# State-space scan: one exponential per direction from a running sum and a per-token offset, masks added on GpSimd, X left unweighted, parts from the states scaled on VectorE

## The reference

```python
xc = (x * dt[..., None]).reshape(bsz, nc, CHUNK, g, r, p)      # 8 chunks of 128 tokens, 4 groups of 6 heads of 64
a = (dt * A).reshape(bsz, nc, CHUNK, g, r).transpose(0, 3, 4, 1, 2)
a_cum = jnp.cumsum(a, axis=-1)
lmat = jnp.exp(segsum(a))                                      # exp(cum[l] - cum[s]) for s <= l, else 0
cb = jnp.einsum('bclgn,bcsgn->bgcls', cc, bc)
y_diag = jnp.einsum('bgcls,bgrcls,bcsgrp->bclgrp', cb, lmat, xc)
...
y_off = jnp.einsum('bclgn,bcgrpn,bgrcl->bclgrp', cc, prev_states, jnp.exp(a_cum))
y = (y_diag + y_off).reshape(bsz, length, g, r, p)
```

## Time and profile before

| what | value |
|---|---|
| median of the runs | 3125.96 us |
| span of the profiled execution | 3120.8 us |
| TensorE busy | 2782.4 us (89%) |
| VectorE busy | 2201.9 us (71%) |
| ScalarE busy | 1268.5 us (41%) |
| GpSimd busy | 771.4 us (25%) |
| loads of the running sums, 768 KB each | 32 |

### The profile page before, as it was taken

How to read it: one execution, slowest core, us unless ns; L and a number is a source line. 1 busy time by engine, 2 the same in 40 slices (tenths; PEclk the granted TensorE clock), 3 DMA queues, 4 the chain that set the end, 5 groups by cost and what they waited for, 6 DMA issues and landing times.

```text
span 3120.8 us, 35706 instructions
## 1 busy us (share of the span) xinstructions
PE 2782.4 (89%) x13124; PEld 2228.8 (71%) x13124; DVE 2201.9 (71%) x2958; ACT 1268.5 (41%) x2069; POOL 771.4 (25%) x389
## 2 busy tenths in 40 slices
PE   6999999989588869979979996989899589999998
PEld 3777776765366658867867884777788468888887
DVE  5599976525688944854644898974465469999997
ACT  2222221110166641123224314666532057777775
POOL 1422220000111100000210005555300036666564
PEclk9999999999788879989989998999999689999999
DMA  6233338643544452226544237341232279999996
GB/s 222 89 108 125 112 118 273 210 150 104 182 165 182 172 213 89 79 78 147 101 119 97 94 89 161 110 120 25 89 122 97 115 285 383 383 382 384 386 383 223
DMA packets 245383, 543.43 MB, mean 174 GB/s; under 512 B 31125, under 2 KB 155141, under 8 KB 228946
## 3 DMA queue, kind: packets, MB, share of 16 engines
q1 hardware_dynamic: 175234, 437.01, 39.6%
q0 software_dynamic: 33680, 58.97, 7.7%
q10 hardware_dynamic: 36288, 45.09, 4.1%
HBM read 450.74 MB, written 108.06 MB: 179 GB/s over the span
## 4 chain that ended last, share of the span: by engine, by line
PE 49%; DVE 8%; POOL 2%; DMA 2%; ACT 2%; issue 1%; SPq 1%; DVEq 0%; ACTq 0%; POOLq 0%; another core or an unknown queue 0%
PE banks L143 44%; PE banks L153 4%; DVE c_rows L1512 2%; DVE a_P L2151 1%; POOL a_P L2175 1%; ACT a_PT L2194 1%; DVE m_w_low L1610 0%; DVE e_low L2654 0%; DMA ofoxT<-a_o 0%; POOL a_R L1545 0%; DMA i_q<-iqT 0%; DVE a_R L1550 0%; ACT m_w_low L1603 0%; DMA p_low_raw<-in_w_out 0%; DMA odsaT<-a_o 0%
## 5 line engine op out<-in xcount | busy, mean ns | idle before, releaser
L2654 DVE TENSOR_TENSOR e_low<-e_raw,e_high 128x4096 fp32r<-128x4096 f32 x99 | 437.9, 4425 | 64.2 <-ACT e_high L2648 64.1
L143 PE MATMUL banks<-m_w_low,p_high 128*128 128x512 f32 (+1 forms) x1280 | 391.7, 390 | 8.5 <-DVE m_w_low L1610 8.5
L2648 ACT ACTIVATE e_high<-e_raw 128x4096 fp32r<-128x4096 f32 x99 | 359.5, 3634 | 27.0 <-DVE e_g L2603 26.9
L143 PE MATMUL banks<-h_high,w 128*128 128x512 f32 (+1 forms) x1088 | 309.3, 368 | 9.0 <-POOL w L373 4.4
L143 PEld LDWEIGHTS banks<-m_w_low,p_high 128*128 128x128 f32 x1280 | 240.0, 194 | 53.0 <-issue 8.7
L143 PE MATMUL banks<-m_w_low,p_low 128*128 128x512 f32 (+1 forms) x640 | 247.2, 386 | 0.0
L143 PEld LDWEIGHTS banks<-h_high,w 128*128 128x128 f32 x1088 | 195.4, 190 | 49.0 <-POOL w L373 4.8
L143 PE MATMUL banks<-e_high,e_xhigh 128*128 128x512 f32 x528 | 211.5, 401 | 7.3 <-issue 5.5
L504 DVE SCALAR_TENSOR_TENSOR acc<-img,taps,acc 128x1024 f32<-128x1024 f32 x160 | 209.8, 1311 | 5.7
L143 PE MATMUL banks<-e_high,e_xlow 128*128 128x512 f32 x528 | 208.3, 394 | 0.0
L143 PE MATMUL banks<-e_low,e_xhigh 128*128 128x512 f32 x528 | 207.8, 394 | 0.0
(11 more groups left out here) (496 smaller groups left out, 6394.9 us busy)
## 6 DMA issues: line engine op xcount, KB each, us to landing
e_raw<-in_exp_w SPq DMA_DIRECT2D x99, 2048.0 KB, 13.9
s_sums<-cumT SPq DMA_DIRECT2D x32, 768.0 KB, 4.3
w_raw<-in_w_in SPq DMA_DIRECT2D x20, 1024.0 KB, 6.5
s_X<-xtok SPq DMA_DIRECT2D x19, 1024.0 KB, 7.3
p_raw<-in_w_in SPq DMA_DIRECT2D x18, 1024.0 KB, 7.0
xbcT<-res ACTq DMA_DIRECT2D x20, 640.0 KB, 2.9
xtok<-xt ACTq DMA_DIRECT2D x20, 640.0 KB, 4.1
w_raw<-in_ada_w SPq DMA_DIRECT2D x12, 1024.0 KB, 5.5
```

The lines of the kernel that those rows point to most:

```text
L143: last = pe.matmul(out, a, b, start=start and n == 0, stop=stop and n == len(pairs) - 1)
L2648: act.activation(self.high[p % HIGHS][:], self.raw[p % RAWS][:], ACT.Copy).then_inc(*self.high_done.up())
L2654: dve.tensor_tensor(self.low[p % HIGHS][:], self.raw[p % RAWS][:], self.high[p % HIGHS][:].bitcast(F32), ALU.subtract).then_inc(*self.low_ ...
```

## The change

In the tables, `gap` and `back` give way to one table `off`: the logarithm of `dt` (no less than 1e-37) minus the running sum, for both directions. The scan's exponentials then take, for each direction by itself, the broadcast running sum plus `off` as bias, so that the result is already the decay times `dt` of the source token. X is used as loaded: `timed` and `xfs` go. There is no minimum of the two exponents any more; what lies outside a direction's triangle is made -1e30 beforehand, by an add of `outside` to both directions' sums on GpSimd (`shut`). The pair products are copied once, without mask, and the weights are one VectorE operation on both directions in place. `scale` moves from ScalarE to VectorE, two operations of 128x384, and gets two buffers. `sums` and `M` have three buffers. The last four steps leave out the state's update, and the last chunk its weighing. The order of the calls changes: the products from the states are made one step ahead, and a step's exponentials two steps ahead; `weights` comes ahead of `gather` and `vector_step`.

```diff
-        dve.tensor_tensor(t["gap"][:], p[:, 0:NT, 0:NH], p[:, 0:NT, NH:2 * NH], ALU.subtract).then_inc(*vec.up())
-        dve.tensor_scalar(t["back"][:], p[:, 0:NT, NH:2 * NH], -1.0, None, ALU.mult).then_inc(*self.tables_done.up())
+        dve.tensor_scalar(self.t["off"][:], self.t["dt"][:, 0:NT, :], TINY, None, ALU.max).then_inc(*vec.up())
+        act.wait_ge(*vec.at(6))
+        act.activation(self.t["off"][:], self.t["off"][:], ACT.Ln).then_inc(*self.logged.up())
...
+        dve.wait_ge(*self.logged.at(1))
+        dve.tensor_tensor(t["off"][:], t["off"][:], p[:, 0:NT, :], ALU.subtract).then_inc(*self.tables_done.up())
...
         def load_sums(n):
-            if n >= 2:
-                sp.wait_ge(*diffed.at(n - 1))
+            if n >= 3:
+                sp.wait_ge(*exped.at(n - 2))
...
+        def shut(n):
+            if n == 0:
+                for w in range(2):
+                    pool.tensor_scalar(outside[:, w, :], MASK[w], -1.0, -FAR, ALU.add, ALU.mult).then_inc(*outlined.up())
+                pool.wait_ge(*outlined.at(2))
+            pool.wait_ge(*sums_in[n % 3].at(n // 3 + 1))
+            pool.tensor_tensor(sums[n % 3][:], sums[n % 3][:], over(outside[:], 2, HG), ALU.add).then_inc(*masked.up())
+
+        def exponents(n):
+            c, g = n // NBC, n % NBC
+            act.wait_ge(*masked.at(n + 1))
+            if n >= 3:
+                act.wait_ge(*summed.at(n - 2))
             for w in range(2):
+                for h in range(HG):
+                    last = act.activation(M[n % 3][:, w, h, :], sums[n % 3][:, w, h, :], ACT.Exp, bias=col("off", c, NH * w + HG * g + h))
+            last.then_inc(*exped.up())
...
-            for w in range(2):
-                last = dve.tensor_tensor(M[n % 2][w][:], E[n % 2][:], over(cbs[c % 2][:, w, g, :], 1, HG), ALU.mult)
-            last.then_inc(*M_done.up())
+            dve.tensor_tensor(M[n % 3][:].rearrange("p w h n -> p (w h) n"), M[n % 3][:].rearrange("p w h n -> p (w h) n"), over(cbs[c % 2][:, g, :], 1, 2 * HG), ALU.mult).then_inc(*M_done.up())
...
         def scale(n):
-            act.wait_ge(*off_summed.at(n + 1))
-            if n:
-                act.wait_ge(*summed.at(n))
+            dve.wait_ge(*off_summed.at(n + 1))
+            if n >= 2:
+                dve.wait_ge(*summed.at(n - 1))
             for w in range(2):
-                for h in range(HG):
-                    at = slice(HP * h, HP * h + HP)
-                    last = act.activation(y2[w][:, at], core.bank[:, y0 + 1 + w, at], ACT.Copy, scale=col("ec", c, NH * w + HG * g + h))
+                last = dve.tensor_tensor(heads(y2[n % 2][w][:]), heads(core.bank[:, y0 + 1 + w, 0:384]), over(col("ec", c, NH * w + HG * g, HG), 2, HP), ALU.mult)
             last.then_inc(*scaled.up())
...
         def vector_step(n):
             dve.wait_ge(*stepping.at(n + 1))
+            dve.wait_ge(*off_summed.at(n + 1))
...
+        load_sums(0), load_chunk(0), load_sums(1)
...
+        load_sums(2), load_chunk(1), load_z(0)
         pool.wait_ge(*rows_in.at(2))
         dve.wait_ge(*rows_in.at(2))
+        tensor_pairs(0), from_states(0), shut(0), shut(1), skip_and_weigh(0), shut(2), skip_and_weigh(1)
+        exponents(0), exponents(1), vector_pairs(0), scale(0), weights(0)
         for n in range(N + 1):
             c, g = n // NBC, n % NBC
-            if n:
-                gather(n - 1), vector_step(n - 1)
             if n < N:
-                from_states(n), scale(n), within_chunk(n), tensor_step(n), both(n)
+                within_chunk(n)
+                if n + 1 < N:
+                    from_states(n + 1)
+                if n < STEPS:
+                    tensor_step(n)
+                both(n)
+            if n + 2 < N:
+                exponents(n + 2)
+            if n + 3 < N:
+                load_sums(n + 3), shut(n + 3)
             if n + 1 < N:
                 weights(n + 1)
-            if n + 2 < N:
-                load_sums(n + 2), differences(n + 2), exponents(n + 2)
+            if n:
+                gather(n - 1)
+                if n - 1 < STEPS:
+                    vector_step(n - 1)
+            if n + 1 < N:
+                scale(n + 1)
             if g == 0 and c:
                 gate(c - 1), roots(c - 1)
...
                 if c + 1 < NT:
                     skip_and_weigh(c + 1)
-            if g >= 2 and c + 1 < NT:
-                timed(g - 2, c + 1)
```

More of the change, by code:

```diff
@@ L995, in state_space @@
         t = {k: s.sb("s_" + k, [P, NT + NC, 2 * NH]) for k in ("dt", "ec", "dec", "et")}
-        t.update({k: s.sb("s_" + k, [P, NT, NH]) for k in ("gap", "back")})
+        t["off"] = s.sb("s_off", [P, NT, 2 * NH])
         Xs = [s.sb(f"s_X{b}", [P, DS + NBC * NST]) for b in range(2)]
@@ L1005, in state_space @@
         xb = [s.sb(f"s_xb{b}", [P, 2 * NBC, P]) for b in range(2)]
[L1006 to L1010, removed]
+        cbs = [s.sb(f"s_cb{b}", [P, NBC, P]) for b in range(2)]
+        sums = [s.sb(f"s_sums{b}", [P, 2, HG, P]) for b in range(3)]
+        M = [s.sb(f"s_M{b}", [P, 2, HG, P]) for b in range(3)]
         yts = [s.sb(f"s_y{b}", [P, DS]) for b in range(2)]
-        y2 = [s.sb(f"s_y2{w}", [P, 384]) for w in range(2)]
+        y2 = [[s.sb(f"s_y2{b}{w}", [P, 384]) for w in range(2)] for b in range(2)]
+        outside = s.sb("s_outside", [P, 2, P])
         sq, skip, nw = s.sb("s_sq", [P, 384]), s.sb("s_skip", [P, NH]), s.sb("s_nw", [P, DS])
@@ L1062, in vector_pairs @@
                 dve.wait_ge(*M_done.at(4 * c - 4))
-            for w in range(2):
[L1064 to L1073, removed]
-            for h in range(HG):
-                last = dve.scalar_tensor_tensor(out=E[n % 2][:, h, :], in0=sums[n % 2][:, 0, h, :], scalar=col("gap", c, HG * g + h),
-                                                in1=sums[n % 2][:, 1, h, :], op0=ALU.subtract, op1=ALU.min)
-            last.then_inc(*diffed.up())
+            dve.tensor_copy(cbs[c % 2][:], core.bank[:, 0, :].rearrange("p (g n) -> p g n", g=NBC)).then_inc(*cb_done.up())
@@ L1082, in exponents @@
-            for h in range(HG):
-                last = act.activation(E[n % 2][:, h, :], E[n % 2][:, h, :], ACT.Exp, bias=col("back", c, HG * g + h))
-            last.then_inc(*E_done.up())
+            act.wait_ge(*masked.at(n + 1))
+            if n >= 3:
+                act.wait_ge(*summed.at(n - 2))
+            for w in range(2):
+                for h in range(HG):
+                    last = act.activation(M[n % 3][:, w, h, :], sums[n % 3][:, w, h, :], ACT.Exp, bias=col("off", c, NH * w + HG * g + h))
@@ L1140, in both @@
             for w in range(2):
-                last = pe.matmul(core.bank[:, 2 + 3 * (n % 2), 0:384], mats[:, C_ID, :], y2[w][:], start=False, stop=w == 1)
+                last = pe.matmul(core.bank[:, 2 + 3 * (n % 2), 0:384], mats[:, C_ID, :], y2[n % 2][w][:], start=False, stop=w == 1)
             last.then_inc(*summed.up())
```

54 lines of the change are left out of this document (21 added, 33 removed).

## The result

The changed kernel takes 3143.27 us (median of four runs, 3136.76 to 3148.31) against 3125.66 in the same comparison: 1.0054 times as long, 95% interval 1.0040 to 1.0069. It is slower by 17.6 us where 4 were forecast (a forecast of 3130 in a range of 3100 to 3156). The profiled execution's span is 3135.1 us, 14.3 over before's 3120.8.

A forecast was written before the change was run, and what follows sets the result against it. VectorE, held by GpSimd, was taken to bound chunk edges, with TensorE needing 24.8 us a chunk. Entry -8.8, chunks +4.2, -2.0, +9.3, +2.2, tail -1.1 and tables 0.1 summed to +3.9: 3130 us, range 3100 to 3156.

The forecast's parts named there:

- The third stall: At a chunk's third step, TensorE waits 3.5 us for a state step delayed behind the roots' ScalarE work.
- The price of an add: GpSimd's mask add of 128x1536, once a step: 2.76 us, from the weighing's row, up to 2.9.
- A steady chunk: Scan chunk: TensorE's 24.8 us, stalls of 2.2, 1.3 and 3.5, up to 1.5 more, and a clock fall: 36.3 us.
- The slow clock: A stall over 3.4 us lets TensorE's clock fall once a chunk, costing another 3 to 4.5 us.
- Chunk 0: Scan's first chunk: GpSimd busy to 856 and stalls of 2.8 and 1.2 us, 33.8 us for 29.6, +4.2.
- rival 3: Two slow clock stretches a chunk, or the first outlasting its stall, and adds of 2.9 us: 3150 us; chance 0.22.
- Chunk 1: Scan's second chunk: no burst of adds at its start, 32.6 us for 34.5, -2.0.
- Chunks 2 to 6: Five steady scan chunks, each 1.84 us longer than before: +9.3 us.
- Chunk 7: Scan's last chunk: no state step, but burst, roots and one slow stretch, 28.8 us for 26.6, +2.2.
- Entry: Scan's start: first product at 843.6 instead of 852.39, -8.8 us.
- Rival 2: GpSimd's adds fall into gaps, only the wait for the roots is left: 29 us a chunk, about 3083; chance 0.13.
- Rival 4: VectorE's PSUM scalings are blocked too, or GpSimd keeps its turn: +40 us, 3170 us; chance 0.05.

The follow-up runs named there:

- e1: The changed kernel with GpSimd's mask add cut to 2 elements a partition, mask and decay weights left out of the result: 28.9 us a chunk.
- e2: The changed kernel with 2-element adds, each behind two GpSimd memsets that write a scratch tile without reading SBUF: 31.6 us a chunk.
- e12: The changed kernel with weights reading pairs from PSUM, state step ahead of weights, and each add in two GpSimd halves: 3084.04 us (0.9877 of before).
- e9: The changed kernel with the weights' product reading the pairs from PSUM, made in the chunk's last step, instead of an SBUF copy: 3144.97 us.
- e10: The changed kernel with pairs read from PSUM by the weights' product, and gather and state step ahead of the weights: 3079.14 us (0.9859 of before).
- e4: The changed kernel with VectorE's weights of the next step put behind gather and state step: 3124.63 us (0.9995 of before).

## Why the prediction was right on the side and short in size

**What bounds the kernel** was read rightly, and so was the path of the loss. GpSimd idle until the store lands, then operations without a gap; weights of 3 to 5 us; PSUM scalings at 0.55; stalls at the state product: all of it is in the timeline above. At the edge of chunk 3 the two state steps ended 5.5 and 16.3 us after the chunk before, where the working has 6.2 and, for the case of a third add, 16; the stalls were 1.53 and 4.62 us for 2.2 and 3.9. The third stall, 3.5 us at the third step behind the roots, did not come: TensorE, late by the second, found that state step done. A stall of 1.62 us stands at the fourth step instead, behind norm, pair copy and weights.

**The price of an add** was wrong. The forecast took 2.76 us from the weighing and set aside its other estimate, 3.4 us, which was the right one: alone an add takes 3.42, and "adds far from 2.8 us" was one of its own signs of being wrong. The weighing's second input is one value repeated over 64 elements, the add's a full row. The trace of the kernel before has such a pair at 128x2048, the first with one value for all elements and the second with a whole tile (shortest, median and longest in ns):

```profile
L371 POOL TENSOR_TENSOR w<-w_raw,zero x13: 3594/3649/3653, 52.7 to 425.9; 128x2048 fp32r<-128x2048 f32 x13
L373 POOL TENSOR_TENSOR w<-w_raw,w x13: 4492/4646/5356, 56.3 to 429.6; 128x2048 fp32r<-128x2048 f32 x13
```

The second row scaled to 1536 elements is 3.4 to 3.5 us, an estimate that could have been made beforehand. No run shows what this term cost by itself. At the edge of chunk 3 the skip product was done 1.2 us sooner than worked out, so part of the good agreement there is luck.

**A steady chunk**: 36.3 us forecast, 35.4 measured as the mean of chunks 2 to 6. Stalls of over 1 us sum to 7.6 us a chunk there, for 7.0 forecast and up to 1.5 more. The slow clock was given 3 to 4.5 us. It took 5.5 us a chunk at half speed with TensorE at work, which costs 2.7. In chunk 3 the clock is 0.52 for 5 us only and then 1.00, where before had 0.50 for 9.6. The forecast tied a slow stretch to one stall of over 3.4 us. That was wrong in itself: the clock fell behind stalls of 1.89 and 2.93 us in chunk 4 and of 2.26 us in chunk 0, and it did not behind one of 2.28 us in chunk 5.

**Chunk 0** is the term that failed most: +4.2 forecast, +11.0 measured (40.6 for 29.6). I had stalls of 2.8 and 1.2 there.

```profile
849.52 5.38 PE L1127 MATMUL banks<-s_X,s_M 128*128 128x64 f32 x24 [15.93 <-DVE s_M L1094]
...
860.67 3.37 DVE L1094 TENSOR_TENSOR s_M<-s_M,s_cb 128x1536 f32<-128x1536 f32 x1 [2.31 <-ACT s_M L1086]
...
868.47 1.62 PE L1158 MATMUL banks<-s_xd,s_X 128*128 128x384 f32 x2 [5.26 <-DVE s_H L1168]
```

They were 5.26 and 2.26 us, 3.5 more in sum. The forecast had GpSimd busy without pause to 856, some 12 us after the first product. In fact three more adds followed at once and kept it busy until 25 us after:

```profile
862.39 12.03 POOL L1076 TENSOR_TENSOR s_sums<-s_sums,s_outside 128x1536 f32<-128x1536 f32 x3
...
864.43 3.31 DVE L1166 TENSOR_TENSOR s_H<-s_H,s_et 128x384 f32<-128x384 f32 x1
...
871.00 5.03 DVE L1094 TENSOR_TENSOR s_M<-s_M,s_cb 128x1536 f32<-128x1536 f32 x1 [1.74 <-ACT s_M L1086]
```

The state step and then the weights were held by them, each ahead of a stall. The other part is the clock, for which the forecast of 33.8 us has nothing beyond before's 29.6 and the two stalls. With TensorE at work it was at half speed for 7.4 us at the chunk's start, for 5.4 after the first stall and for 3.4 after the second, 16.2 us in all where before had 8.9: another 3.7 us.

```profile
849.50:856.90 7.40, 7.38 (x28) 6.47 (x29) 4.20 (x1) 0.00 (x0) 7.40 (x2) 0.50 0.28 107
868.50:873.90 5.40, 5.40 (x13) 3.58 (x14) 3.66 (x3) 3.62 (x13) 5.40 (x2) 0.50 0.35 112
880.80:884.20 3.40, 3.40 (x7) 1.74 (x6) 3.29 (x3) 0.00 (x0) 3.21 (x1) 0.50 0.02 5
```

This is rival 3, more than one slow stretch in a chunk. Chunks 2 and 4 had two slow stretches as well, but of 3 to 4 us each, together no longer than the one that the forecast had counted.

**Chunk 1**: -2.0 forecast, +1.9 measured (36.4 for 34.6), with a stall of 4.70 us in its third step. The weights there came late behind the roots. Without the adds (e1) that leaves a stall of 2.2 us. Here the weights met the end of a single add, and the state step met the weighing:

```profile
906.41 2.15 DVE L1094 TENSOR_TENSOR s_M<-s_M,s_cb 128x1536 f32<-128x1536 f32 x1 [5.04 <-ACT s_M L1086]
...
906.89 4.28 POOL L1148 TENSOR_TENSOR s_xd<-s_X,s_dec 128x1536 f32<-128x1536 f32 x1
...
908.95 2.65 DVE L1166 TENSOR_TENSOR s_H<-s_H,s_et 128x384 f32<-128x384 f32 x1
...
912.33 1.62 PE L1158 MATMUL banks<-s_xd,s_X 128*128 128x384 f32 x2 [4.70 <-DVE s_H L1168]
```

I had taken it that without a burst there is little hold. A single instruction is enough where the state step stands behind it. What followed cost more than the stall: the clock was at half speed until 925.1, 12.8 us of TensorE's work.

```profile
912.40:925.00 12.60, 12.60 (x36) 9.23 (x37) 7.63 (x14) 3.62 (x12) 6.21 (x3) 0.50 0.39 149
```

That is the second term that failed. **Chunks 2 to 6**: +9.3 forecast, +5.0 measured. **Chunk 7**: +2.2 and +2.3. **Tail**: -1.1 and -0.85.

**Entry**: from the scan's rows landing to the first product -7.9 us (11.95 for 19.83), forecast -8.8. It didn't show in full in the span: the scan began its loads 4.3 us later, and the rows took 0.7 more to land.

```profile
823.17 0.37 SPq L1037 DMA_DIRECT2D s_sums<-cumT  x1
...
837.57 0.67 POOL L1073 TENSOR_SCALAR s_outside<-mats 128x128 f32<-128x128 f32 x2 [159.83 <-DMA s_nw<-in_ssd_norm_w]
```

In the stage ahead the granted clock from 710 to 720 us is 0.84 in this execution and 1.00 in before's. It isn't the change as such: among the twelve profiles whose code ahead of the scan is the changed kernel's, the scan's loads begin between 817.3 us (e1) and 825.0 (e2), and before's begin at 818.9. Why they differ stays open. The two mask operations took 0.67 us together, 0.6 forecast.

**The sum**: -2.9 at the first product, +11.0, +1.9, +5.0, +2.3, -0.9, and some -2 in the later stages, which the change leaves alone, make about 14.3, the difference of the spans. Against the forecast's +3.9 that is 6.8 more in chunk 0, 3.9 in chunk 1 and 5.9 before the first product, 4.3 less in chunks 2 to 6, and the 2 of the later stages, which I had not counted. The median is 3.3 us further off than this profile, which is within the spread of the runs. That the side came out right owes something to luck: slower had a chance of 0.41 against 0.34 for faster, and the terms that failed went both ways.

**The rivals.** Rival 2 (the adds fall into gaps, 29 us a chunk) didn't happen, but its floor was right: without the adds a chunk took 28.9 us. TensorE's own 24.8 us is borne out too; the shortest chunks of e12 took 25.9 and 26.0. Rival 4 (GpSimd keeps its turn, or PSUM scalings are blocked) is excluded by 0.55 us beside adds, and by the products that VectorE got in between three adds in a row. The Trainium skill (SBUF — State Buffer, Who interferes with whom) says that a VectorE instruction with at most one input in SBUF, outside its two-port modes, doesn't contend with GpSimd. By that rule the way out could have been read before the change was made; the 1.75 us of the weights in e9 and e10, beside adds as without them, agree.

I did not name in the forecast what e4 showed: that the change also moved the weights ahead of the state step in VectorE's queue, and that this alone costs 18.6 us once the weights can be held. The working of each stall had the weights first, but I never asked what the other order would give.

## What to carry to other kernels

Before you move elementwise work from VectorE to GpSimd, count the VectorE products with both inputs in SBUF that will run beside it, charge each with up to one GpSimd instruction, and charge GpSimd's instructions with the VectorE ones: here the adds cost as much on GpSimd as on VectorE (35.6 and 35.9 us a chunk). Take the price of the GpSimd instruction from a row with the same kind of inputs: the add took 3.42 us where another product of its size took 2.76. Where one of the inputs comes out of PSUM anyway, read it there; and in a queue that is held now and then, put first what the busiest engine waits for. The two moves have to be weighed together: against the changed kernel the read from PSUM alone gave +2 us (nothing clear of the noise), the order alone -19, and both -64.

## What the runs showed of the hardware that I had not expected

- The exclusion costs GpSimd as well: adds that take 3.42 us alone took up to 4.95, 4.1 in the mean, and three in a row 13.57.
- A held product of VectorE lost less than one GpSimd instruction, even in a burst of three: 3.3 us at most (5.03 for weights of 1.75) beside adds of 3.42, and 2.56 (4.31) beside the skip product of 2.76. The two engines took turns.
- A GpSimd instruction on 128x1536 fp32 took 2.76 us where its second input repeats one value per head, and 3.42 where it is a full row.
- GpSimd writing SBUF without reading it (memsets) left VectorE's products at 1.75 us; theory A1 of e2 had that.
- The length of a stall did not tell the length of the slow stretch behind it. After a stall of 4.62 us in chunk 3 the granted clock was near half (0.52) for 5 us only, after one of 4.70 us in chunk 1 it was 0.50 for 12.8 us, and after one of 3.45 us in the kernel before for 9.6 us.
